# Products of zeros while TensorE waits between the sub-layers of a two-layer streaming encoder

## The reference

```python
for l in range(DEPTH):                                   # 2
    mod = (cs @ ada_w[l] + ada_b[l]).reshape(bn, N_SUB, 3, D_MODEL)
    shift, scale, gate = ...
    u = x * (1.0 + scale[:, 0]) + shift[:, 0]
    y = _swiglu(u, ffn_w13[l, 0], ffn_w2[l, 0])          # FFN, inner width 2816
    x = _layer_norm(ALPHA * x + 0.5 * gate[:, 0] * y, ln_g[l, 0], ln_b[l, 0])
    u = x * (1.0 + scale[:, 1]) + shift[:, 1]
    y = _hybrid_mixer(u, w_in[l], w_out[l], ...)         # two attentions, mLSTM, S5
    x = _layer_norm(ALPHA * x + gate[:, 1] * y, ln_g[l, 1], ln_b[l, 1])
    u = x * (1.0 + scale[:, 2]) + shift[:, 2]
    y = _swiglu(u, ffn_w13[l, 1], ffn_w2[l, 1])
    x = _layer_norm(ALPHA * x + 0.5 * gate[:, 2] * y, ln_g[l, 2], ln_b[l, 2])
```

## Time and profile before

| | |
|---|---|
| device time, median of 3 runs | 1294.12 us (1293.29 to 1294.85) |
| span of the profiled execution | 1289.0 us |
| PE busy | 1124.2 us (87%) |
| DVE busy | 997.0 us (77%) |
| ACT, POOL busy | 404.3 us (31%), 238.3 us (18%) |
| mean granted clock of PE | 0.943 |

### The profile page before, as it was taken

How to read it: one execution, slowest core, us unless ns; L and a number is a source line. 1 busy time by engine, 2 the same in 40 slices (tenths; PEclk the granted TensorE clock), 3 DMA queues, 4 the chain that set the end, 5 groups by cost and what they waited for, 6 DMA issues and landing times.

```text
span 1289.0 us, 19845 instructions
## 1 busy us (share of the span) xinstructions
PE 1124.2 (87%) x7103; PEld 976.0 (76%) x7103; DVE 997.0 (77%) x1436; ACT 404.3 (31%) x508; POOL 238.3 (18%) x217
## 2 busy tenths in 40 slices
PE   1399899989978789999959979997997878999995
PEld 1298789967765379999949878996775537999994
DVE  6779998883894588888568999888389458888857
ACT  0234323421223133333323432432122313333331
POOL 1005910013131120000030590002223112000003
PEclk9999989999988979999979998999998897999997
DMA  8798588961430368887655758886143046888730
GB/s 293 240 318 279 191 289 286 319 171 66 98 98 6 144 220 284 294 310 276 220 181 185 263 200 286 287 317 159 66 99 98 21 144 223 281 289 314 261 132 33
DMA packets 206179, 265.59 MB, mean 206 GB/s; under 512 B 42046, under 2 KB 145650, under 8 KB 206108
## 3 DMA queue, kind: packets, MB, share of 16 engines
q1 hardware_dynamic: 206108, 264.69, 61.2%
HBM read 263.62 MB, written 1.05 MB: 205 GB/s over the span
## 4 chain that ended last, share of the span: by engine, by line
issue 71%; POOL 12%; PE 8%; DVE 7%; DMA 1%; SPq 0%; ACT 0%; POOLq 0%; DVEq 0%
PE PS L553 5%; POOL sin_t L1605 2%; DVE arena L1079 2%; POOL rot_flat L1602 2%; POOL rot_flat L1601 1%; POOL cos_t L1604 1%; POOL rot_flat L1600 1%; POOL x_sb L1581 1%; POOL rot_flat L1599 1%; DMA x_sb<-in_x_dram 1%; PE PS L560 1%; POOL x_sb L1583 1%; POOL arena L1618 1%; POOL arena L1619 1%; DVE xn L950 1%
## 5 line engine op out<-in xcount | busy, mean ns | idle before, releaser
L464 PE MATMUL PS<-u_hi,w_in_hi 128*128 128x256 f32 x1408 | 404.3, 287 | 12.4 <-DVE u_lo L840 7.4
L465 PE MATMUL PS<-u_lo,w_in_hi 128*128 128x256 f32 x1408 | 400.8, 285 | 0.0
L466 PE MATMUL PS<-u_hi,w_in_lo 128*128 128x256 f32 x1408 | 400.1, 284 | 0.0
L464 PEld LDWEIGHTS PS<-u_hi,w_in_hi 128*128 128x128 f32 x1408 | 274.2, 195 | 19.4 <-DVE u_lo L840 10.1
L465 PEld LDWEIGHTS PS<-u_lo,w_in_hi 128*128 128x128 f32 x1408 | 269.6, 191 | 3.3 <-issue 1.9
L466 PEld LDWEIGHTS PS<-u_hi,w_in_lo 128*128 128x128 f32 x1408 | 269.1, 191 | 0.0
L889 DVE TENSOR_TENSOR w_in_lo<-w_in_ring,w_in_hi 128x2048 fp32r<-128x2048 f32 x88 | 208.1, 2366 | 36.3 <-ACT w_in_hi L1356 36.3
L810 DVE SCALAR_TENSOR_TENSOR acc<-arena,cs,acc 128x512 f32<-128x512 f32 x273 | 217.7, 797 | 9.7
L1356 ACT ACTIVATE w_in_hi<-w_in_ring 128x2048 fp32r<-128x2048 f32 x88 | 167.7, 1910 | 19.8 <-PE PS L748 16.2
L480 PE MATMUL PS<-w_out_hi,h_parts 128*128 128x512 f32 x352 | 146.0, 415 | 17.8 <-DVE h_parts L883 17.8
L1364 ACT ACTIVATE w_out_hi<-w_out_ring 128x1024 fp32r<-128x1024 f32 x88 | 88.4, 1053 | 199.8 <-PE PS L484 194.9
(11 more groups left out here) (269 smaller groups left out, 1246.4 us busy)
## 6 DMA issues: line engine op xcount, KB each, us to landing
w_in_ring<-in_ffn_w_dram SPq DMA_DIRECT2D x88, 1024.0 KB, 7.5
arena<-in_ada_w_dram SPq DMA_DIRECT2D x39, 2048.0 KB
w_out_ring<-in_ffn_w_dram SPq DMA_DIRECT2D x44, 1024.0 KB, 6.5
w_in_ring<-in_w_in_dram SPq DMA_DIRECT2D x8, 1024.0 KB, 5.5
work_flat<-in_ada_w_dram SPq DMA_DIRECT2D x3, 2048.0 KB
w_out_ring<-in_w_out_dram SPq DMA_DIRECT2D x4, 1024.0 KB, 6.8
w_in_ring<-in_w_in_dram SPq DMA_DIRECT2D x2, 2048.0 KB, 8.8
w_out_ring<-in_w_out_dram SPq DMA_DIRECT2D x8, 512.0 KB, 4.5
```

What stands on the lines that cost most here:

```text
L464: pe.matmul(y, hi, u_hi[:, kt, :], start=(i == 0), stop=False)
L465: pe.matmul(y, hi, u_lo[:, kt, :], start=False, stop=False)
L466: mm = pe.matmul(y, lo[:, kt, half, :], u_hi[:, kt, :], start=False, stop=(i == KT - 1))
```

## The change

A new function on PE, `idle_y(count)`, makes products of zeros with the same operands as `seed_y`, all into bank 0 of y, each one complete in itself (start and stop). It is called in `turn` ahead of each half's wait for `xn`, six times in the first half and eight in the second, and, eight more, in front of `seed_y` in both FFNs. The ones in `turn` wait for DVE's first read of bank 0 (`y_read`). The first `turn`, in front of the loop, has none.

```diff
+            def idle_y(count):
+
+                for k in range(count):
+                    pe.matmul(PS[:, 0, :], zeros_bf[0:1, 0:P], zeros_bf[0:1, :], start=True, stop=True)
+
             def turn(src, l, s):
 
                 for tt in range(2):
                     if s is not None:
+                        pe.wait_ge(sem("y_read"), l * 12 + (4 * s + 5))
+                        idle_y((6, 8)[tt])
                         pe.wait_ge(sem("xn_act"), l * 6 + (2 * s + tt + 1))
                         if tt == 1:
                             pe.wait_ge(sem("xn_dve"), l * 3 + (s + 1))
...
             with pe.Fori(0, DEPTH) as l:
 
                 pe.wait_ge(sem("y_read"), l * 12 + 4)
+                idle_y(8)
                 seed_y()
                 ffn_chunk(l, 0, 0, 0)
...
                 pe.wait_ge(sem("y_read"), l * 12 + 12)
+                idle_y(8)
                 seed_y()
                 for j in range(2):
                     ffn_chunk(l, 1, 0, j)
```

## The result

The changed kernel takes 1299.81 us (median of 6 runs, 1296.47 to 1301.68) against 1293.70 (1292.23 to 1295.96) of the kernel before, run beside it. The ratio is 1.0041, with a 95% interval of 1.0027 to 1.0054: 5.3 us slower (3.5 to 7.0). The forecast was 1298.0, 3.9 us slower. The measured median lies in the range for 8 in 10 (1292.0 to 1300.5) and above my own narrower one (1297.0 to 1299.2).

A forecast was written before the change was run, and what follows sets the result against it. PE, busy 87% of the span, was taken as the bound. 3.4 (head of layer 1) + 0.3 (transposes ahead) + 0.2 (end) = +3.9 us, giving 1298.0; own range 1297.0 to 1299.2, 8 in 10 1292.0 to 1300.5.

The forecast's parts named there:

- Zeros of one row don't hold the clock: In all seams: products with one row count little or nothing for PE's clock; mean clock unchanged near 0.94.
- The head of layer 1, +3.4: In front of seed_y at layer 1's start: nothing covers the eight products at low clock, 3.4 us on the path.
- The transposes ahead of it, +0.3: Out of a second FFN: eight products need 3.4 us where 2.97 are free, so about 0.3 us late.
- The end, +0.2: After layer 1: little of the kernel hangs on the late transposes; 0.2 us for DVE's last instructions.
- The second FFN's eight, 0: In front of a second FFN: the wait for u_lo hides the products, with 0.4 us to spare.
- The mixers' seams, 0: Into the mixer: six cost 0; eight cost 1.8 to 3.4 against 3.18 us free, taken as nothing.
- A seam's delay passes on: In the FFN behind layer 1's head: its chunks follow PE, so nothing gives the delay back.
- a rival at 0.10: Mixer's seam at low clock: fall before the first transposes, up to 1.8 us late per layer, 1301.6; chance 0.10.
- What lies around the span: Whole kernel: the median lies 5.1 us above the profiled span, so span 1292.9 gives 1298.0.
- The rival that zeros count: Second FFNs and layer 1's head: zeros count as activity, clock up sooner; sum -1.4, 1292.7; chance 0.13.

The follow-up runs named there:

- head alone: Kernel before plus only eight one-row products of zeros in front of seed_y at the head of each layer; ratio 1.0018 (1.0007 to 1.0028), 2.3 us.
- the head left out: Changed kernel without the eight products of zeros at the head of the layers; ratio to the kernel before 1.0021 (1.0010 to 1.0033), 2.7 us.
- `seed_y` early: Kernel before with the next layer's seed_y moved ahead of the last seam's transposes and the loop's jump, nothing added; ratio 0.9991 (0.9980 to 1.0001).
- 128 rows and none at the head: Changed kernel with idle products over 128 rows of zeros and none at the head of the layers; 1291.24 us, ratio 0.9971 to the kernel before.

## Why the prediction was right, point by point

- **Zeros of one row don't hold the clock: right, and shown.** I read it from a fall in the midst of nearly gapless work of few rows. In the changed kernel the clock stays at 0.50 from 285 to 291 with PE busy 3.00 of 3.00 us twice, and 128 rows turn it round.
- **The head of layer 1, +3.4: right.** 3.4 us on the timeline of the changed kernel, 3.5 with the head alone, 2.3 (0.9 to 3.6) in the time. The first FFN behind it, from read to read, is 3.6 us longer in the changed kernel and 3.9 with the head alone, so nothing gave it back. That u_lo would have been ready only 0.9 us earlier was not in my sum, and not needed for it.
- **The transposes ahead of it, +0.3:** measured 0.5.
- **The end, +0.2:** measured 0.0, 22.74 before and 22.75 after.
- **The second FFN's eight, 0: right.** 19.25 before, 19.26 after. The margin of 0.4 us was 0.3.
- **The mixers' seams, 0: the step that was mis-sized.** "Into the mixer there are 3.18 us; ... so eight cost between 1.8 and 3.4: from nothing to 0.3 late, and I take nothing", and "Cost 0" for the six. They took 3.1 and 0.6 in the changed kernel's profile and 2.7 us in the time with the head left out. I priced both groups at the clocks of the one profile that I had, where the fall came after the first transposes, and kept the fall ahead of them as a rival at 0.10, "up to 1.8 us late, per layer". It happened in one of two seams in the profile of the changed kernel, and cost 3.1. The free time was too large in the sum: it took in all of the 1.81 us of idle time ahead of the first transposes, but PE still waits for ACT's cT there, and the six start only 0.87 us after it went idle. From there the six, the first transposes and the eight have 5.05 us, and took 8.1 at the low clock. Nor does it take a fall ahead of the transposes: in the four mixer seams with the six over one row the fall came at 6.2 to 9.2 us and the seams are 3.1, 1.6, 1.4 and 0.6 longer, 1.7 on average, so some 3.3 us for two layers stood in the sum as 0. In the six such seams without zeros ahead of the transposes (before, head alone, `seed_y` early) the fall came at 8.4 to 9.5, so the one profile of before could not show this spread.
- **A seam's delay passes on: right.** The two parts measured apart make 2.3 and 2.7 us, 5.0 of the 5.3. That the number came out within the range was in part luck: 2.7 us stand where the sum has 0.5 (0.3 and 0.2), and the head's 3.4 measured 2.3 in the time, which its interval does not tell from 3.4.
- **What lies around the span:** I took 5.1 us; it is 1.8 in the changed kernel and 1.7 to 3.1 in the one before. The profiled execution of before was a fast one. The forecast was made as a difference and did not suffer, but the share of the seams in the two spans would have misled me.
- **The rival that zeros count fell.** Its 1.7 us for each second FFN was too much as well: with the clock held by 128 rows the 96th product came 0.1 to 0.3 us earlier, since u_lo binds. The Trainium skill, "TensorE: Matmul & The Clock Gate", Why this matters for your kernels, gives no idle gaps as the rule. This case's traces agree only for products over 128 rows: over one row PE was busy without a gap from 283.14 to 293, and the clock stayed at 0.50.

## What to carry to other kernels

Filler work on an engine is free only where a wait on the path behind it is longer than the filler at the slowest clock it may meet; behind a loop's jump, where the first instruction waits for nobody, every product counts. If filler is meant to keep PE's clock up, give it all 128 rows (zeros did here), look at the granted clock and not at the busy share, and leave out the places where it can't be hidden: here that turned +5.3 us into -3.8. A clock that falls inside a seam need not fall at the same point in each execution (6.2 to 9.5 us after the seam's start here), so price the seam at both clocks. And follow a gain to the end of the next stretch: 5.1 us won in the seams left 1.0 in the span of the profiled execution.

## What the runs showed of the hardware

- PE busy without a gap for 10 us, most of it products over one row, stayed at the low clock (0.50 from 285 to 291); the same products, zeros as well, over 128 rows kept it at 1.00 up to the mixer's start, or to 0.5 us ahead of it, in all eight mixer seams, 64 rows in one seam of two, 32 in neither. Duration and pitch of a product don't depend on its rows: six took 1.46 with one row and with 32, 1.47 with 128, at full clock.
- Faster transposes moved work between DVE and POOL. The kernel before, in front of layer 0's second FFN:

```profile
455.05 2.50 DVE L851 CAST u_hi<-uT_lo 128x512 fp32r<-128x512 f32 x1
...
457.47 3.44 DVE L840 TENSOR_TENSOR u_lo<-uT_lo,u_hi 128x512 fp32r<-128x512 f32 x2
```

and the kernel with 128 rows and none at the head:

```profile
454.00 0.66 DVE L859 CAST u_hi<-uT_lo 128x512 fp32r<-128x512 f32 x1
454.34 2.52 POOL L1589 TENSOR_TENSOR x_sb<-xn,ln_bc 128x1024 f32<-128x1024 f32 x1
...
454.58 5.60 DVE L848 TENSOR_TENSOR u_lo<-uT_lo,u_hi 128x512 fp32r<-128x512 f32 x2
```

The cast takes 0.66 us where it starts ahead of POOL's L1589. It takes 2.50 where it starts 0.12 us behind the same instruction (L1581 in the kernel before, at 454.93 for 2.34 us), and then it ends 0.28 us after that one. In the other order the two subtractions behind the cast take 5.60 us instead of 3.44. That PE could start 2.3 us earlier in the second FFN, and then wait, seems to hang on this order. That DVE and POOL hinder each other is what the durations suggest; no run here took POOL's work away.
